# Mixer C's first projection group takes the sample's token tiles first, and the copies that reorder the prompt's activations are spread over four units

## The reference

```
h = rms_norm(x, ln_g) * (1 + scale) + shift
A: q, k, v = h @ w_in[...]   -> differential attention, 4 heads
B: q, k, v = h @ w_in[...]   -> neighbourhood attention on a (rows x 64) grid, 8 heads
C: q, k, v = h @ w_in[...]   -> dilated sliding windows, 3 groups of 4 heads, mixed by their denominators
each mixer: u_i = sigmoid(h @ w_g[i]) * ((y_i * silu(h @ w_z[i])) @ w_br[i])
out = (u_A + u_B + u_C) @ w_out;   x = x + gate * out
```

## Time and profile before

| what | value |
|---|---|
| median of 3 runs | 2401.92 us (2400.65 to 2403.06) |
| the profiled execution, its own time | 2400.95 us |
| its span (first to last instruction) | 2399.1 us |
| PE busy | 2364.6 us, 99% of the span |
| PEld busy | 2115.8 us, 88% |
| DVE busy | 1403.5 us, 58% |
| ACT busy | 1035.7 us, 43% |
| chain that ended last | PE 90%, DVE 4%, ACT 4%, issue 1%, DMA 1% |
| PE's granted clock in 40 slices | 0.9 or more in each |

### The profile page before, as it was taken

The page is one execution under the profiler, slowest core; times in us unless marked ns, Lnnn a source line. Parts: engine busy times, 40 slices in busy tenths (PEclk is TensorE's granted clock), DMA queues, the critical chain, the costliest instruction groups (busy, mean ns, idle before and its releaser), DMA issues.

```text
span 2399.1 us, 41217 instructions
## 1 busy us (share of the span) xinstructions
PE 2364.6 (99%) x15754; PEld 2115.8 (88%) x15754; DVE 1403.5 (58%) x4032; ACT 1035.7 (43%) x2835; POOL 58.5 (2%) x103
## 2 busy tenths in 40 slices
PE   7999999999999999999999999999999999999999
PEld 5788888889899999888888888888988999998888
DVE  6876425775356676643478853277643676765432
ACT  5666414663134444432356662256531444444220
POOL 0010001200000000000001000021000000000000
PEclk9999999999999999999999999999999999999999
DMA  7221212112111111321420111212121111122123
GB/s 275 93 74 36 80 66 94 48 49 76 61 55 44 57 55 58 115 77 54 157 83 34 45 45 66 73 35 62 42 77 66 44 55 58 55 83 89 66 67 123
DMA packets 50931, 173.48 MB, mean 72 GB/s; under 512 B 8240, under 2 KB 21168, under 8 KB 48304
## 3 DMA queue, kind: packets, MB, share of 16 engines
q1 hardware_dynamic: 40800, 157.70, 18.6%
q10 hardware_dynamic: 9936, 13.15, 1.6%
HBM read 162.44 MB, written 6.29 MB: 70 GB/s over the span
## 4 chain that ended last, share of the span: by engine, by line
PE 90%; DVE 4%; ACT 4%; issue 1%; DMA 1%; SPq 0%; DVEq 0%; ACTq 0%
PE ps_proj L719 75%; PE ps_pt L875 2%; PE ps_score L862 2%; PE ps_pv L910 2%; PE ps_score L847 1%; PE ps_pv L892 1%; PE ps_tr L925 1%; PE ps_tr L926 1%; PE ps_pv L904 1%; ACT act_hi L1119 1%; DMA w_raw<-in_w 1%; ACT probs L1241 1%; PE ps_score L853 1%; DVE top L1598 1%; PE ps_proj L767 0%
## 5 line engine op out<-in xcount | busy, mean ns | idle before, releaser
L719 PE MATMUL ps_proj<-w_hi,act_hi 128*128 128x384 f32 x1824 | 631.8, 346 | 2.7 <-DVE w_lo L1789 1.3
L719 PE MATMUL ps_proj<-w_hi,act_lo 128*128 128x384 f32 x1824 | 611.8, 335 | 0.0
L719 PE MATMUL ps_proj<-w_lo,act_hi 128*128 128x384 f32 x1824 | 611.6, 335 | 0.0
L719 PE MATMUL ps_proj<-act_hi,w_hi 128*128 128x256 f32 (+1 forms) x1312 | 443.4, 338 | 0.0
L719 PE MATMUL ps_proj<-act_lo,w_hi 128*128 128x256 f32 (+1 forms) x1312 | 441.8, 337 | 0.0
L719 PE MATMUL ps_proj<-act_hi,w_lo 128*128 128x256 f32 (+1 forms) x1312 | 441.1, 336 | 0.0
L719 PEld LDWEIGHTS ps_proj<-w_hi,act_hi 128*128 128x128 f32 x1824 | 342.8, 188 | 7.5 <-issue 2.2
L719 PEld LDWEIGHTS ps_proj<-w_lo,act_hi 128*128 128x128 f32 x1824 | 343.4, 188 | 0.0
L719 PEld LDWEIGHTS ps_proj<-w_hi,act_lo 128*128 128x128 f32 x1824 | 342.5, 188 | 0.0
L1205 ACT ACTIVATE sig<-ps_proj 128x512 f32<-128x512 f32 (+1 forms) x144 | 70.6, 491 | 501.7 <-PE ps_proj L719 500.2
L1789 DVE TENSOR_TENSOR w_lo<-w_raw,w_hi 128x1536 fp32r<-128x1536 f32 (+2 forms) x168 | 272.3, 1621 | 16.7 <-ACT w_hi L1043 16.4
(11 more groups left out here) (195 smaller groups left out, 3400.6 us busy)
## 6 DMA issues: line engine op xcount, KB each, us to landing
w_raw<-in_w SPq DMA_DIRECT2D x128, 768.0 KB, 4.4
w_raw<-in_w SPq DMA_DIRECT2D x40, 512.0 KB, 3.9
w_ada<-in_w_mod SPq DMA_DIRECT2D x11, 1536.0 KB, 6.5
first_ada<-in_w_first SPq DMA_DIRECT2D x8, 1024.0 KB, 12.5
out_y<-merged ACTq DMA_DIRECT2D x16, 256.0 KB, 2.0
merged<-in_x_in SPq DMA_DIRECT2D x8, 384.0 KB, 6.2
x_old<-in_x_in ACTq DMA_DIRECT2D x8, 256.0 KB, 4.2
out_y<-merged ACTq DMA_DIRECT2D x16, 128.0 KB, 3.7
```

The source lines that it names most:

```text
L719: op = pe.matmul(out, sta[s](k), mov[m](k), start=(k == 0 and n == 0), stop=(k == chunks - 1 and n == 2))
```

## The change

C's first group now goes through tiles 4, 5, 0, 1, 2, 3. The attentions it opens stay those of tiles 0 to 5 of B's head 3, in this order. Moves 0 to 2 are done in the pass of ("B", 3, 0, 4), 3 to 5 in that of ("B", 3, 0, 5), 6 and 7 in that of ("C", 0, 0, 4), and move 8 in that of ("C", 0, 0, 5), always at the end of the pass. PE waits once, for move 8, at the start of ("C", 0, 0, 0), which is now the group's third unit. Since C's v of tiles 4 and 5 goes straight into a buffer in which B's head 2 has its v, ACT's copy of it for tile 4 now waits for the value products of B's head 2, tile 5.

```diff
+def tiles_in_order(kind, h, g):
+
+    return (4, 5, 0, 1, 2, 3) if (kind, h, g) == ("C", 0, 0) else range(TILES)
...
-        for t in range(TILES):
+        for t in tiles_in_order(kind, h, g):
             out.append(("q", l, kind, h, g, t))
...
-MOVES = {("B", 3, 0, 4): range(0, 4), ("B", 3, 0, 5): range(4, 7), ("C", 0, 0, 0): range(7, KC + 1)}
+MOVES = {("B", 3, 0, 4): range(0, 3), ("B", 3, 0, 5): range(3, 6), ("C", 0, 0, 4): range(6, KC),
+         ("C", 0, 0, 5): range(KC, KC + 1)}
...
-            return (l, "A" if kind == "B" else "B", 3, t)
+            return (l, "A" if kind == "B" else "B", 3, tiles_in_order(kind, h, g).index(t))
...
-                    if u == ("q", l, "C", 0, 0, 0) and k < KC - 1:
-                        pe.wait_ge(*hi_moved.at((l, k + 2)))
-                        pe.wait_ge(*lo_moved.at((l, k + 2)))
...
                 if u == ("q", l, "C", 0, 0, 0):
-                    pe.wait_ge(*hi_moved.at((l, 1)))
-                    pe.wait_ge(*lo_moved.at((l, 1)))
+                    pe.wait_ge(*hi_moved.at((l, KC)))
+                    pe.wait_ge(*lo_moved.at((l, KC)))
...
+                    if (kind, h, g, t) == ("C", 0, 0, 4):
+
+                        act.wait_ge(*pv_ready.at((l, "B", 2, 5)))
                     act.activation(dst, made(u, 256, 384), ACT.Copy).then_inc(*act_read.inc(u))
...
-                if u == ("q", l, "C", 0, 0, 0):
-                    for i in MOVES[u[2:]]:
-                        move_high(l, i)
...
-                if u[0] == "q" and u[2] == "B":
+                if u[0] == "q":
                     for i in MOVES.get(u[2:], ()):
                         move_high(l, i)
```

More of the change, by code:

```diff
@@ L967, in between @@
                             turn_unit(u2)
-                    if u == ("q", l, "C", 0, 0, 0) and k < KC - 1:
-                        pe.wait_ge(*hi_moved.at((l, k + 2)))
-                        pe.wait_ge(*lo_moved.at((l, k + 2)))
                     if u == ("q", l, "A", 0, 0, JOINT) and k < KC - 1:
                         pe.wait_ge(*lo_ready.at((l, 1, k + 1)))
-                    if u[0] == "q" and u[5] == 0 and k == 3:
+                    if u[0] == "q" and u[5] == tiles_in_order(*u[2:5])[0] and k == 3:
                         pe.wait_ge(*w_lo_ready.at(pieces_of(u)[1]))
@@ L978, in _ @@
                 if u == ("q", l, "C", 0, 0, 0):
-                    pe.wait_ge(*hi_moved.at((l, 1)))
-                    pe.wait_ge(*lo_moved.at((l, 1)))
+                    pe.wait_ge(*hi_moved.at((l, KC)))
+                    pe.wait_ge(*lo_moved.at((l, KC)))
                 if u[0] == "q":
                     _, _, kind, h, g, t = u
-                    if t == 0:
+                    if t == tiles_in_order(kind, h, g)[0]:
                         pe.wait_ge(*w_lo_ready.at(pieces_of(u)[0]))
@@ L1802, in _ @@
                     dve.wait_ge(later_in, 16 * 4)
-                if u == ("q", l, "C", 0, 0, 0):
-                    for i in MOVES[u[2:]]:
-                        move_low(l, i)
                 if u3 is not None and u3[0] == "a":
```

## The result

| what | before | after |
|---|---|---|
| median of 19 runs each | 2401.16 us (2399.88 to 2404.96) | 2406.07 us (2402.00 to 2409.10) |
| ratio, 95% interval | | 1.0017 (1.0010 to 1.0023) |
| the profiled execution, its own time | 2400.95 us | 2406.07 us |
| its span | 2399.1 us | 2404.3 us |
| mean granted clock of PE | 0.999 | 0.998 |

The time is 4.9 us higher by the medians. That is 0.2%: small, but the whole interval lies above 1. The forecast of 2404.0 was 2.1 too low and its range (2401.2 to 2407.6) holds the result. The range of the runs has grown too: from 5.1 us wide to 7.1.

The account below looks back on a forecast made before the run. PE, busy 99% of the span, was taken as the bound, with 5.7 us lost around the moves. A later third C unit, +1.0 a layer, gave 2401.92 + 2.1 = 2404.0 us, range 2401.2 to 2407.6.

Parts of the forecast that it names:

- The first two C units run free: C's first two units in each layer: they read sample columns only, so no wait for moves; worth 0.4 a layer.
- The wait for move 8, +1.0 a layer: Third C unit: move 8 stands behind two more ACT passes, so its scores come at 500.1 instead of 499.10.
- One sign: ACT at layer 0's moves: it would run without a gap from 475.24 to about 498.9, move 8 last.
- ACT's added wait costs nothing: ACT's v copy of tile 4: value products at about 491, ACT there at 493.52, so no cost while ACT is late.
- The value DMAs are hidden: Tile 3's five v DMAs ahead of a weight load: it lands at 531.6, hidden with 4.7 us to spare.
- Nothing else is lost behind move 8: Behind the third C unit's start: ACT is level with PE again and nothing more is won or lost.
- The likeliest case: Whole kernel: the forecast case, +1.0 a layer and +2.1 us in all, 2404.0 us, chance 0.54.
- the clock rival: PE behind the wait for move 8: clock halves, 1.7 a layer; both layers 2407.4 (chance 0.18), one 2405.7 (0.13).
- order term: Third C unit's later start from the new order of work: +1.0 a layer, +2.1 us over both.

Follow-up runs that it names:

- one layer left unfilled: Changed kernel with 18 needless PE products ahead of the wait for move 8 in one layer only: layer 0 2404.74 us, layer 1 2403.87 us.
- the fillers: Changed kernel with needless PE products ahead of the wait for move 8 in both layers: 18 products 2401.66 us, 9 products 2402.46 us.
- 4/3/1/1: Changed kernel with four moves in the first pass, then three, one and one, move 8 still last: 2401.67 us, ratio 1.0007.
- 4/3/2: Changed kernel with four, three and two moves, all done before the second C unit's pass: 2396.52 us (0.9983), once more 2397.11 us (0.9989).

## Why the prediction was right in part, point by point

- *The first two C units run free.* Right: three stretches of 6.19 or 6.20, no wait for a move, for turned q and k, for probabilities or for a bank.
- *The wait for move 8, +1.0 a layer.* Right in mechanism, over-sized by 0.4. Third unit's first product stands 497.48 - 470.36 = 27.12 behind the scores of ("B", 3, 0, 4); before it is 499.10 - 1.14 - 471.46 = 26.50. So it is **+0.62** (layer 1: +0.65). The chain from move 0 to this product was put at 23.70 and took 23.34. Both C passes fit to 0.02 (3.99 and 4.77). What was over-sized are the rows of moves: a row with a square behind it hands over some 0.1 before the end that I had reckoned (3.57, 3.49 and 2.30 for 3.67, 3.62 and 2.40), and the pass behind the first row, set by DVE, was 0.1 shorter. Against it, PE started 0.1 later behind move 8. The wait was forecast at 3.3 to 3.8 and is 3.3 and 3.4. One sign did not hold: ACT was to run without a gap from move 0 to move 8, but it stands six times for DVE's sums and maxima, 4.2 us in all (0.67, 0.69, 0.32, 0.69, 0.32, 1.49). Waits of 0.32, 0.69 and 1.49 stand in the passes of the kernel before too, so "ACT has no rest" was a misreading; it cost the sum nothing, since each pass was taken over whole, with its waits in it.
- *ACT's added wait costs nothing.* Right, no idle time ahead of the copy at 492.24.
- *The value DMAs are hidden.* Right. The next weight load goes out at 527.78, and ACT splits the piece at 536.43 with no idle time ahead of it; this is 1.18 behind the earlier trace rows, of which the third unit and the clock explain all (-1.1 + 0.6 + 1.7 = 1.2).
- *Nothing else is lost behind move 8.* **This step failed.** I gave the fall of the clock 0.31 as a rival, 0.18 for both layers, against 0.54 for none. What I had put at nothing behind the third unit's start was the larger part of the loss: 1.7 and 2.8 us in the trace, against 0.6 a layer for the later unit. Both traces of the changed kernel, and those with one layer left unfilled, show a fall at each rest of 3.3 us: six of six. Its price was right in layer 0 (1.7 forecast, 1.7 measured) and too small in layer 1 of the changed kernel (2.8), where it fell during the rest and lasted twice as long. The Trainium skill, "TensorE: Matmul & The Clock Gate", section "Why this matters for your kernels", tells to leave no long idle gap between bursts; the traces agree for 3.3 us, with 1.7 to 2.8 us lost each time, and show a fall behind some shorter rests as well (two of five near 2.1 us, three of thirty of 1.6 to 1.8).
- *The time.* The likeliest case said +2.1 us. What happened is +1.3 for the order, by the traces, and some 4 for the clock: 4.9 and 5.7 less 1.3 leave 3.6 and 4.4. The range holds 2406.07 because its upper end was drawn for the clock rival (2407.4), and the likeliest case came within 2.1 us partly by luck: its order term was 0.8 too large over both layers, and it started from 2401.92 where the kernel before has 2401.16. The runs scatter: the lowest, 2402.00 at a mean granted clock of 0.999, is where the order alone would be (2401.16 + 1.3 = 2402.5), and the highest, 2409.10, has 0.996. Only the traced executions show where the clock fell; that it is the same in the other runs is inferred from their mean clocks and from the fillers.

## What to carry to other kernels

In these traces no fall followed a wait of 0.3 to 0.7 us at the moves, and one followed each wait of 3.3 us: if a wait on the full engine can't be avoided, split it or put work into it, and look at the granted clock behind every rest from 1.7 us up. When a dependent chain of copies is put behind other passes, count how many passes stand ahead of its *last* link; where the others lie matters less (0.33 us a layer between 3/3/2/1 and 4/3/1/1). And before work is taken out of the first row of a late engine, look whether the other engine keeps it waiting there anyway: if it does, part of that room is free.

## What the runs showed that was not expected

- The clock can fall within the rest itself, and dense products of 128x384 on both sides of the rest did not prevent it. Each fall lasted 3.4 us, except the two that began within a rest of 3.3 us, which lasted 6.8.
- There is no sharp line between harmless and harmful rests: the same rest of 1.7 us (ended between 1256 and 1262 us) was followed by a fall in three traces and by none in nine, and of two rests of 2.1 us in one execution only the second was. Longer rests were hit more often. What decides in a single case is not shown.
- Falls away from the moves add to the scatter of the times: two of them cost some 3.4 us in the second trace of 4/3/2 (2399.83 us, that kernel's slowest run of eleven), and none is in the first (2396.3).
- 18 products a layer that compute nothing which is kept made the program 4 to 5 us faster: they run while PE would have stood anyway, and prevent falls that cost 1.7 and 2.8 us in the trace.
